# Layer-step kernel with product-key experts: routing stage with query weights loaded in halves, zero-adds in place of casts, and a rearranged end

## The reference, cut to what matters

```python
def peer(h, wq, keys, u, v):
    q = (x @ wq).reshape(t, 8, 2, 128)              # 8 heads, 2 halves
    sc = jnp.einsum('thpc,hpnc->thpn', q, keys)     # 128 keys per half
    s_top, i_top = lax.top_k(sc, 16)
    cand = s_top[:, :, 0, :, None] + s_top[:, :, 1, None, :]
    cs, ci = lax.top_k(cand, 16)
    i1 = take(i_top[:, :, 0], ci // 16); i2 = take(i_top[:, :, 1], ci % 16)
    idx = i1 * 128 + i2                             # one of 16384 experts
    g = softmax(cs)
    a = gelu(einsum(u[idx], x)) * g
    return einsum(a, v[idx])
```

## Time and profile before

| | us |
|---|---|
| median of 3 runs | 3171.96 (3168.54 to 3177.21) |
| the profiled execution | 3170.31 |
| its span, first to last instruction | 3167.9 |
| PE busy | 3001.9 (95%) |
| DVE busy | 2797.2 (88%) |
| POOL busy | 1892.7 (60%) |
| ACT busy | 1210.3 (38%) |

### The profile page before, as it was taken

How to read it: one execution, slowest core, us unless ns; L and a number is a source line. 1 busy time by engine, 2 the same in 40 slices (tenths; PEclk the granted TensorE clock), 3 DMA queues, 4 the chain that set the end, 5 groups by cost and what they waited for, 6 DMA issues and landing times.

```text
span 3167.9 us, 48593 instructions
## 1 busy us (share of the span) xinstructions
PE 3001.9 (95%) x15946; PEld 2501.8 (79%) x15946; DVE 2797.2 (88%) x5568; ACT 1210.3 (38%) x2077; POOL 1892.7 (60%) x1387
## 2 busy tenths in 40 slices
PE   7998987889999999999999898789999999999998
PEld 6856654479999999999997455579999999999997
DVE  3474597989999999999998689989999999999998
ACT  3332355633333333333333347633333333333333
POOL 1000166767677887776663058767777776777663
PEclk9999999999999999999999899999999999999999
DMA  5231366799999999999997446789999999999995
GB/s 238 72 133 49 136 237 266 295 378 409 408 407 409 403 407 385 410 409 401 409 398 269 185 171 266 304 333 406 409 410 399 409 401 387 409 395 410 408 402 223
DMA packets 248698, 1049.33 MB, mean 331 GB/s; under 512 B 23056, under 2 KB 72976, under 8 KB 205840
## 3 DMA queue, kind: packets, MB, share of 16 engines
q0 software_dynamic: 147456, 536.94, 43.0%
q1 hardware_dynamic: 99408, 460.72, 37.4%
q10 hardware_dynamic: 1728, 50.33, 3.7%
HBM read 994.68 MB, written 53.22 MB: 331 GB/s over the span
## 4 chain that ended last, share of the span: by engine, by line
PE 83%; DVE 11%; DMA 3%; issue 1%; ACT 1%; POOL 1%; DVEq 0%; SPq 0%; ACTq 0%
PE bankA L1713 11%; PE bankA L1711 11%; PE bankA L1712 11%; PE bankD L1724 7%; PE bankD L1725 7%; PE bankD L1723 7%; PE bankA L1671 4%; PE bankA L1725 4%; PE bankA L1724 4%; PE bankA L1723 4%; DVE hot L1420 2%; DMA wch<-in_wq 2%; PE bankD L1912 1%; PE bankD L1926 1%; PE bankA L1775 1%
## 5 line engine op out<-in xcount | busy, mean ns | idle before, releaser
L1711 PE MATMUL bankA<-hh,uh 128*128 128x384 f32 x2048 | 687.1, 335 | 1.7 <-DVE ul L1471 1.7
L1713 PE MATMUL bankA<-hh,ul 128*128 128x384 f32 x2048 | 687.4, 336 | 0.0
L1712 PE MATMUL bankA<-hl,uh 128*128 128x384 f32 x2048 | 685.9, 335 | 0.0
L709 POOL DMA_INDIRECT hT<-in_u,idxc x320 | 449.6, 1405 | 171.6 <-issue 76.1
L709 POOL DMA_INDIRECT hT<-in_v,idxc x320 | 440.7, 1377 | 182.2 <-issue 67.1
L857 ACT ACTIVATE wt<-bankA 128x384 f32<-128x384 f32 x256 | 126.0, 492 | 1046.3 <-PE bankA L1713 808.3
L1487 DVE SCALAR_TENSOR_TENSOR wch<-hT,a,wch 128x1024 f32<-128x1024 f32 x320 | 399.3, 1278 | 7.0 <-DMA hT<-in_v,idxc 5.2
L1724 PE MATMUL bankD<-vl,wh 128*128 128x512 f32 x1024 | 399.8, 390 | 0.0
L1725 PE MATMUL bankD<-vh,wl 128*128 128x512 f32 x1024 | 399.3, 390 | 0.0
L1723 PE MATMUL bankD<-vh,wh 128*128 128x512 f32 x1024 | 398.3, 389 | 0.0
L1478 DVE CUSTOM_DVE_ANT_0 hT<-hT,htok 128x1024 f32<-128x1024 f32 x320 | 383.1, 1221 | 15.6 <-DMA hT<-in_u,idxc 9.7
(11 more groups left out here) (255 smaller groups left out, 5618.5 us busy)
## 6 DMA issues: line engine op xcount, KB each, us to landing
uraw<-in_uT SPq DMA_DIRECT2D x128, 1024.0 KB
vraw<-in_vP SPq DMA_DIRECT2D x128, 1024.0 KB
wch<-in_wq SPq DMA_DIRECT2D x34, 2048.0 KB, 8.4
gates_scratch<-gbuf ACTq DMA_DIRECT2D x12, 4096.0 KB, 14.1
wch<-gates_scratch SPq DMA_DIRECT2D x64, 768.0 KB
wch<-in_ada SPq DMA_DIRECT2D x19, 2048.0 KB, 8.7
wch<-in_qkv SPq DMA_DIRECT2D x3, 2048.0 KB, 23.6
adap<-in_ada SPq DMA_DIRECT2D x3, 2048.0 KB, 15.8
```

What stands on the lines that cost most here:

```text
L709: pool.indirect_dma_start(out=row_buf[slot], out_offset=None, in_=table.rearrange("l e d -> (l e) d"), in_offset=bass.IndirectOffsetOnAxis ...
L1711: pe.matmul(abank[c], hi, hh[:, k, :], start=k == 0, stop=False)
L1712: pe.matmul(abank[c], hi, hl[:, k, :], start=False, stop=False)
L1713: last = pe.matmul(abank[c], lo, hh[:, k, :], start=False, stop=k == K - 1)
```

## The change

- **Modulation products.** In layer 0 six of eight now stand at the ends of units 3 to 8, and two come after "htok"; in layer 1 the two stand at the ends of units 5 and 7. "htok" moves to step 4 of unit 9, right after the last gates and their store.
- **Query weights in halves.** Each chunk of `wq` is loaded as two transfers of 1 MB. The first half may start once the first half of the chunk in its buffer has been used (`q_half`), if that one is a query chunk as well; the second half waits for the whole use as before. PE waits for the halves separately, before parts 0 and 2.
- **Short copies as sums.** The casts at L1314, L1346 and L1361 become sums with 64 zeros kept in PSUM.
- **Memory.** `hh`, `hl` and `htok` now lie over the first half of `gbuf`, `uraw` and `vraw` over the second; the waits for `stored[0]` and `stored[1]` are exchanged accordingly, on SP and on ACT.
- **Rests.** POOL forms `hl` in eight instructions of 384 elements instead of one of 3072.
- **Folds.** The last mask is folded on DVE by three sums of halves (1024, 512 and 256 elements), and two of 64, instead of two reductions over 1024 elements.
- PE also waits for `idx_ready` ahead of its idle products, which are three now.

```diff
-            if L == 0 and 4 <= u < UNITS - 1 and r == PER_UNIT - 1 or u == UNITS - 1 and r % 2:
+            if u == UNITS - 1 and r == 4:
+                o.append(("htok", L))
+            if FIRST_HOT <= u < UNITS - 1 and r == PER_UNIT - 1 and (L == 0 or u % 2 and u > FIRST_HOT):
                 o += next_ada()
     while len(done) < len(late):
         o += next_ada()
-    return o + [("adat",) + late[-1][1:], ("htok", L)]
+    return o + [("adat",) + late[-1][1:]]
...
+                hh = sb("hh", [P, K, TD], F32R, where=dn)
+                hl = sb("hl", [P, K, TD], F32R, where=dn)
+                htok = sb("htok", [P, GT, D], where=dn)
                 uraw = sb("uraw", [P, 2, 2 * D], where=dn)
                 vraw = sb("vraw", [P, 2, 2 * D], where=dn)
-                hh = sb("hh", [P, K, TD], F32R, where=dn)
-                hl = sb("hl", [P, K, TD], F32R, where=dn)
-                htok = sb("htok", [P, GT, D], where=dn)
...
+        zeros = bankD[0][:, 896:896 + HALF * TOPK]
...
-                sp.wait_ge(stored[0], 16 * ((L + 1) * DT + 1))
+                sp.wait_ge(stored[1], 16 * ((L + 1) * DT + 1))
                 for p in range(2):
                     load_u(L, p, p)
                 for p in range(2):
                     load_v(L, p, p)
-                sp.wait_ge(stored[1], 16 * ((L + 1) * DT + 1))
+                sp.wait_ge(stored[0], 16 * ((L + 1) * DT + 1))
...
             for n, (name, last) in enumerate(chunks):
+                if name[0] == "wq" and chunks[n - 2][0][0] == "wq":
+                    sp.wait_ge(q_half, SECOND[chunks[n - 2][1]])
+                    sp.dma_start(wch[:, n % 2, 0:K * CH // 2], source(name)[:, 0:K * CH // 2]).then_inc(half_ready[n % 2], 16)
...
-                sp.dma_start(wch[:, n % 2, 0:src.shape[1]], src).then_inc(chunk_ready[n % 2], 16)
+                if name[0] == "wq":
+                    if chunks[n - 2][0][0] != "wq":
+                        sp.dma_start(wch[:, n % 2, 0:K * CH // 2], src[:, 0:K * CH // 2]).then_inc(half_ready[n % 2], 16)
+                    sp.dma_start(wch[:, n % 2, K * CH // 2:K * CH], src[:, K * CH // 2:K * CH]).then_inc(chunk_ready[n % 2], 16)
+                else:
+                    sp.dma_start(wch[:, n % 2, 0:src.shape[1]], src).then_inc(chunk_ready[n % 2], 16)
...
-                pool.tensor_tensor(hl[:, :, :], hT[:, :, 0:TD], hh[:, :, :].bitcast(F32), ALU.subtract
-                                   ).then_inc(h_split, 1)
+                for k in range(K):
+                    last = pool.tensor_tensor(hl[:, k, :], hT[:, k, 0:TD], hh[:, k, :].bitcast(F32), ALU.subtract)
+                last.then_inc(h_split, 1)
...
-                        act.wait_ge(stored[1], 16 * ((L + 1) * DT + 1))
+                        act.wait_ge(stored[0], 16 * ((L + 1) * DT + 1))
...
-                    v.tensor_copy(topf[:, 1, :, :], topi[:, 1, :, :])
+                    v.tensor_tensor(topf[:, 1, :, :], topi[:, 1, :, :], heads(zeros), ALU.add)
...
-                    narrowed = mark(v.tensor_copy(ci, csi[:, :, :].rearrange("p t k -> p (t k)")))
+                    narrowed = mark(v.tensor_tensor(ci, csi[:, :, :].rearrange("p t k -> p (t k)"), zeros, ALU.add))
...
-                        v.tensor_copy(base, topi[:, 0, :, 0:1])
+                        v.tensor_tensor(base, topi[:, 0, :, 0:1], heads(zeros)[:, :, 0:1], ALU.add)
...
+                v.memset(zeros, 0.0)
...
+                m3 = mask[:, :, :, :, :].rearrange("p c t a k -> p (c t) (a k)")
+                for n in (8 * TOPK, 4 * TOPK, 2 * TOPK):
+                    then(v.tensor_tensor(m3[:, :, 0:n], m3[:, :, 0:n], m3[:, :, n:2 * n], ALU.add))
                 for c in range(2):
-                    last = v.tensor_reduce(heads(i12[:, t % 2, c, HALF * TOPK:PH * TOPK]), mask[:, c, :, :, :].rearrange("p t a k -> p t k a"), AX.X, ALU.add)
+                    last = v.tensor_tensor(heads(i12[:, t % 2, c, HALF * TOPK:PH * TOPK]), mask[:, c, :, 0, :],
+                                           mask[:, c, :, 1, :], ALU.add)
...
                         if part == 0:
-                            rows = chunk(whole)
+                            b = CN[whole] % 2
+                            pe.wait_ge(half_ready[b], 16 * HALVES[whole])
+                            rows = wch[:, b, :].rearrange("p (k n) -> p k n", n=CH)
+                        if part == 2:
+                            pe.wait_ge(chunk_ready[b], 16 * (CN[whole] // 2 + 1))
...
+                        if part == 1:
+                            last.then_inc(q_half, 1)
...
                 pe.wait_ge(htok_ready, (L + 1) * GT)
-                keep_warm(5)
                 pe.wait_ge(h_split, L + 1)
+                pe.wait_ge(idx_ready, (L + 1) * GT)
+                keep_warm(3)
```

More of the change, by code:

```diff
@@ L264, in build @@
         CN[unit] = CN[first_use]
+    QUERY = [c[0] for c in chunks if c[0][0] == "wq"]
+    USE = {c[0]: c[1] for c in chunks}
+    HALVES = {}
+    for name in QUERY:
+        b = CN[name] % 2
+        HALVES[name] = 1 + sum(CN[other] % 2 == b for other in QUERY[:QUERY.index(name)])
+    for unit, first_use in SHARED.items():
+        HALVES[unit] = HALVES[first_use]
+    SECOND = {}
+    for L in range(DEPTH):
+        for unit in route_order(L):
+            if unit[0] == "wq" and unit[4] == 1:
+                SECOND[unit[0:4]] = len(SECOND) + 1
     with ExitStack() as ctx:
@@ L367, in build @@
             with ExitStack() as dn:
-                uraw = sb("uraw", [P, 2, 2 * D], where=dn)
-                vraw = sb("vraw", [P, 2, 2 * D], where=dn)
                 hh = sb("hh", [P, K, TD], F32R, where=dn)
@@ L372, in build @@
                 htok = sb("htok", [P, GT, D], where=dn)
+                uraw = sb("uraw", [P, 2, 2 * D], where=dn)
+                vraw = sb("vraw", [P, 2, 2 * D], where=dn)
                 uh = sb("uh", [P, 2, D], F32R, where=dn)
@@ L411, in build @@
         pads_zeroed = sem("pads_zeroed")
+        half_ready = [sem(f"half_ready{i}") for i in range(2)]
+        q_half = sem("q_half")
         chunk_ready = [sem(f"chunk_ready{i}") for i in range(2)]
```

## The result

The changed kernel takes 3150.83 us (median of 4 runs, 3150.03 to 3154.49) against 3171.43 us (4 runs) for the kernel before: a ratio of 0.9937, 95% interval 0.9923 to 0.995. The gain is 20.6 us where 47.8 were forecast, and 3150.8 lies above the range of 3108 to 3141.

The account below looks back on a forecast made before the run. Predicted bound: DVE paces layer 1's router, waits for PE and late query weights hold layer 0's, PE the dense stage; -25.0 - 16.2 - 10.0 - 2.6 + 6.0 = -47.8 us from 3170.3 gives 3122.5 us, range 3108 to 3141.

Parts of the forecast that it names:

- Halves: Layer 0's router: query weights in halves remove DVE's 29.0 us of waits, 4 us may stay; gain 25.0 us.
- The first rival: Layer 0's router stays held by PE; 10.2 us of waits plus 8.1 of casts, 3141 us; chance 0.13.
- The prediction's own sign of being wrong: Layer 0's router: the prediction is wrong if one-hots still wait for PE over 10 us.
- The first rival's other reason: Layer 0's router: PE busy 28.8 us with a modulation, a DVE unit about 28.6, so no room.
- Sums with zeros: Both routers, units 3 to 8: twelve casts on DVE get 1.35 us shorter each; gain 16.2 us.
- The lower bound: Gain from the casts made sums if PE holds layer 0: 8.1 us instead of 16.2.
- The end: Last mask to first scan takes 8.8 us in both layers; gain 10.0 us in layer 0, 2.6 in layer 1.
- the early last store: Router end: last store starts 15.8 us before the last mask is done, lands after 12.3 at best, leaving 3.5 us.
- POOL's pieces: Router ends: pieces delay DVE at row numbers, 16-bit shift and a wait between masks and products; 3 us per layer.
- The rival with all pieces paid: Router ends: DVE pays all eight pieces in both layers, 16 instead of 6 us, 3132.5 us; chance 0.10.
- The moved products of layer 1: Layer 1's units 5 and 7: two modulations, 3 us of PE each, cost nothing while three `hot` slots hold.
- the rival that would have been slower: Dense stage turns DMA-bound and PE waits at every pair; costs 64 us, 3186 us; chance 0.04.

Follow-up runs that it names:

- zeros_only: The kernel before with only the three casts as sums with zeros in PSUM; 3165.9 us, ratio 0.9984 to before.
- casts_back: The changed kernel with its three sums with zeros as casts again; 3160.4 us, ratio 0.9954 to the kernel before.
- places_before: The changed kernel with the modulation products back at their old places in both layers; 3155.3 us, one run.
- small_store: The changed kernel with only an eighth of each store of gates made (512 KB instead of 4 MB); 3124.7 us, one run.
- end_only: The kernel before with the rearranged end alone, without moved modulation products, halves and zeros; 3177.4 us, ratio 1.002 to before.
- zeros_sbuf: The changed kernel with the first of the three sums taking its zeros from SBUF instead of PSUM; 3157.8 us, one run.
- halves_only: The kernel before with the query chunks loaded in halves and nothing else; 3159.9 us, ratio 0.9965 to before.

## Why the prediction was wrong

**Halves, booked -25.0, measured -11.1.** This is the step that failed: "With the wait gone, DVE's 29.0 us go". It took an early issue for an early landing. The prediction said that the first half starts "some 7 us earlier", which was right (7.3 us by the modulation chunk's issue in the case above), and never asked what else is in the DMA engines then, though the issue times of the store and the modulation chunk could be read from the trace. The half lands after 15.7 us where 10.8 had served for twice as much, so PE's wait only shrinks from 23.1 to 15.4 us. The first rival had just this ("a half that lands late, with 4 MB stores ... beside it"), and a chance of 0.13. It priced it at 10.2 us for the waits; the part alone lost 25.0 - 11.1 = 13.9. That the one-hots' wait is 29.3 us after, and not the 19.3 of the halves alone, has two further causes in the record: the 8.1 us that the sums save DVE in layer 0 come back as waiting (+6.9 in zeros_only; 6.1 less with casts_back), and the new places of the modulation products add about 3 (25.9 in places_before). The prediction's own sign of being wrong, one-hots waiting over 10 us, came true. The first rival's other reason, PE's own work, is not what held layer 0: small_store has the same work and reaches 273.5 us, 39.8 less than before where 40.1 were forecast.

**Sums with zeros, booked -8.1 in each layer, measured 0 to -3 in layer 0 and -6.1 (alone) to -8.1 (first sum only) in layer 1.** The size and the mechanism were right. The condition "once PE no longer holds layer 0" failed with the halves. The lower bound, 8.1 for one layer, was near the right value.

**The end, booked -10.0 and -2.6, measured -10.0 and -2.2.** Step for step: row numbers done 4.6 us after the last mask in both layers (4.5 said), six records of idle products 4.59 and 5.46 us (4.3 said), scan at 8.8 and 9.25 us (8.8 said). The end alone is a loss, however (end_only), and so is the end with the old places (places_before): in both the last store is issued 14.0 us before the last mask is done, and in the changed kernel, where it is 18.9 us, the loss is absent. The prediction named the early last store as its margin.

**POOL's pieces, booked +3 per layer; measured 0.25 at the row numbers and 3.3 at the candidate sums.** The size was right and the reason wrong: three pieces were booked at three places, and four were paid at one. "It waited for all of them and did not slip in between" was read from high parts of 2.23 us that began after DVE's sums; where POOL's pieces are already running, pieces and sums alternate. The rival with all pieces paid did not come about. Masks and the 16-bit shift lost nothing (0.68 and 0.18 us).

**The moved products of layer 1, booked 0, measured +4.4** (places_before), 4.3 us of it as two waits of the one-hots, the longer 2.3 us, which places_before doesn't have. "Nothing, while the three slots hold": they did not hold, since PE also waited 2.9 us for halves there and then restarted.

**The sum again.** Layer 0: -11.1 + 0 - 10.0 + 3.6 = -17.5, measured -15.8; the 1.7 us between them may be the new places of layer 0, which cost 3.5 us by places_before (one run). Layer 1: by zeros_only and zeros_sbuf -6.1 to -8.1, + 4.4 - 2.2 + 3.6 - 1.5 for the halves there (halves_only) = -1.8 to -3.8, measured -3.5. Of the error of 28 us the late landing accounts for some 22: 13.9 us directly and 8.1 of casts behind it; with the small stores layer 0's router gets 24.0 us back. The moved products of layer 1 are 4.4 more. The dense stages stayed as they were, so the rival that would have been slower did not come about.

## What to carry to other kernels

Starting a load earlier gains only as much as it lands earlier. List what else is in the DMA engines at the new time, with issue times and sizes, and estimate the landing from the bytes under way over the measured rate; moving the consumer to where the engines are free (here half a unit) can be worth more than issuing earlier. A saving on an engine counts only where that engine sets the pace after the change, so when one term makes room for another, the second term is conditional and belongs into the same case. And where DVE and POOL share a stretch, put one operand of DVE's short sums in PSUM and cut POOL's long instructions.

## What the runs showed of the hardware

- A load of 1 MB, issued 6.2 us behind one of 2 MB and 2.5 us behind a store of 4 MB, took 15.7 us, where the median of such halves is 5.4. In the kernel before 2 MB, issued 9.8 us behind such a store, took 10.8. With the store cut to 0.5 MB no such half took over 7.4. The smaller transfer had no precedence, and being on another queue than the store did not help it.
- A sum of 128x64 elements took 0.21 us with one input in PSUM and 1.58 us with both in SBUF while POOL worked on 1024 elements per partition; without POOL 0.21 us for both.
- Exclusion goes by instruction. Eight pieces of 0.96 us let DVE's sums in one at a time (3.87 us for four, against 0.62), one piece of 6.65 us held one operation for 6.18 us, and MAX8 and FIND_INDEX8, which read a single SBUF tile, were not held up by the pieces (0.60 us for four and 0.21 us, as without POOL). That does not go for every operation with one SBUF input: the cast beside POOL's high part took 1.55 us instead of 0.18.
